# A fused attention stage: v as the stationary operand, pairs of query tiles, and probabilities scaled before they are turned

## The reference, cut to what matters

```python
s = einsum('bqhd,bkhd->bhqk', q, k) * ATT_SCALE
s = where(mask, s + cq - ck, -inf)            # causal; c: running sums of log forget values
o = einsum('bhqk,bkhd->bqhd', softmax(s), v)
...
merged = sigmoid(g_att) * (att @ w_pa) + sigmoid(g_ssm) * (y_ssm @ w_pb)
x = x + merged @ w_out                        # then an MLP
```

## Time and profile before

| what | value |
|---|---|
| median of 3 executions | 2892.29 us (2890.13 to 2892.56) |
| the profiled execution, its own time | 2892.2 us |
| its span, first to last instruction | 2890.4 us |
| mean granted TensorE clock | 0.982 of full |
| PE busy | 2782.0 us (96%) |
| DVE, ACT, POOL busy | 1653.6, 902.5, 251.4 us |
| attention stage | from about 400 to 1314 us of the span |
| branches stage | from about 1696 to 1930 us |

### The profile page before, as it was taken

The page is one execution under the profiler, slowest core; times in us unless marked ns, Lnnn a source line. Parts: engine busy times, 40 slices in busy tenths (PEclk is TensorE's granted clock), DMA queues, the critical chain, the costliest instruction groups (busy, mean ns, idle before and its releaser), DMA issues. The chain is left out here.

```text
span 2890.4 us, 48919 instructions
## 1 busy us (share of the span) xinstructions
PE 2782.0 (96%) x19338; PEld 2711.1 (94%) x19338; DVE 1653.6 (57%) x3203; ACT 902.5 (31%) x2161; POOL 251.4 (9%) x379
## 2 busy tenths in 40 slices
PE   6998979999999999997999989998989999999999
PEld 5997979999999999997999989998989999999999
DVE  4336337667667676676898854464373444344434
ACT  4223325444444444442434331121231111111110
POOL 0000000000000000003555520000000000000000
PEclk8999989999999999998999999999989999999999
DMA  3222232132222231325888863343121111111112
GB/s 115 90 90 56 76 90 91 44 100 78 72 86 82 74 93 52 91 73 135 208 198 207 204 188 116 111 138 123 63 104 55 48 45 44 44 45 44 47 67 95
DMA packets 339091, 273.38 MB, mean 95 GB/s; under 512 B 111824, under 2 KB 315216, under 8 KB 338736
## 3 DMA queue, kind: packets, MB, share of 16 engines
q1 hardware_dynamic: 338864, 270.26, 32.5%
HBM read 197.90 MB, written 72.28 MB: 93 GB/s over the span
## 5 line engine op out<-in xcount | busy, mean ns | idle before, releaser
L401 PE MATMUL banks<-w_hi,xn_hi 128*128 128x256 f32 x1440 | 405.0, 286 | 8.4 <-DVEq L357 5.0
L401 PE MATMUL banks<-w_lo,xn_hi 128*128 128x256 f32 x1440 | 402.0, 284 | 0.0
L404 PE MATMUL banks<-xn_hi,w_hi 128*128 128x352 f32 x1152 | 380.0, 330 | 0.0
L404 PE MATMUL banks<-xn_hi,w_lo 128*128 128x352 f32 x1152 | 377.4, 328 | 0.0
L404 PE MATMUL banks<-xn_lo,w_hi 128*128 128x352 f32 x1152 | 376.8, 327 | 0.0
L401 PE MATMUL banks<-w_hi,xn_lo 128*128 128x256 f32 x1280 | 363.1, 284 | 0.0
L401 PEld LDWEIGHTS banks<-w_hi,xn_hi 128*128 128x128 f32 x1440 | 274.3, 191 | 10.0 <-DVEq L357 5.1
L401 PEld LDWEIGHTS banks<-w_lo,xn_hi 128*128 128x128 f32 x1440 | 273.9, 190 | 0.6
L1683 PE MATMUL banks<-h_hi,w_hi 128*128 128x352 f32 x768 | 248.9, 324 | 1.9 <-DVEq L1604 1.9
L1683 PE MATMUL banks<-h_hi,w_lo 128*128 128x352 f32 x768 | 248.7, 324 | 0.0
L1683 PE MATMUL banks<-h_lo,w_hi 128*128 128x352 f32 x768 | 248.7, 324 | 0.0
(11 more groups left out here) (281 smaller groups left out, 6219.8 us busy)
## 6 DMA issues: line engine op xcount, KB each, us to landing
w_raw<-in_w_in SPq DMA_DIRECT2D x44, 1024.0 KB, 5.5
scratch_xbc<-att_co SPq DMA_DIRECT2D x32, 512.0 KB, 2.6
ssd_ab<-scratch_acum SPq DMA_DIRECT2D x64, 256.0 KB, 6.0
br_g<-scratch_gates SPq DMA_DIRECT2D x72, 176.0 KB, 2.5
scratch_gates<-hand_tanh SPq DMA_DIRECT2D x48, 176.0 KB, 5.1
scratch_z<-att_z_stage SPq DMA_DIRECT2D x64, 128.0 KB, 1.9
ssd_xbc<-scratch_xbc SPq DMA_DIRECT2D x64, 128.0 KB, 3.3
ssd_xbc<-scratch_xbc SPq DMA_DIRECT2D x128, 64.0 KB, 3.7
```

The lines of the kernel that those rows point to most:

```text
L401: ins = self.nc.tensor.matmul(self.bank(n, P, PW), x[:, k, t * P:(t + 1) * P], w[:, k, :], start=first, stop=end)
L404: ins = self.nc.tensor.matmul(self.bank(n, P, TT), w[:, k, m * P:(m + 1) * P], x[:, k, r * TT:(r + 1) * TT], start=first, stop=end)
```

## The change

The turned probabilities become the moving operand, and v_hl the stationary one, so that one load of v serves two query tiles. The unit of work is now a pair of query tiles (u = 0 to 3: tiles 2u and 2u + 1; u = 4, LASTU, is tile 8 alone). For a pair the blocks of both tiles are turned into one bank: four transposes to a full group (2 key blocks by 2 tiles), three to the diagonal one. The product comes out turned, [128, 256] for a pair: rows 0 to 63 are the high part of v, rows 64 to 127 the low one; ACT copies one half and DVE adds the other (64 partitions). As the row sum now lies along the free dimension of the output, it can't be applied there: POOL multiplies `pr` by it in place before the turning, after DVE has inverted it. A projection tile is cut in three parts (8 matmuls each), and a unit has three slots with the numbers of parts in `share`. att_d becomes [D, T], and branches reads its blocks without transposes.

```diff
-        size = len(passes) // parts
-        for c in range(part * size, (part + 1) * size):
+        for c in range(part * len(passes) // parts, (part + 1) * len(passes) // parts):
...
+        if s == 0:
+            sp.dma_start(self.blocks(u), self.att_d[:, tokens].rearrange("(k p) t -> p k t", p=P)).then_inc(self.rows_loaded[j], 16)
...
-                sp.wait_ge(turned, 2 * (u - 2))
+                if u - handed.ROWS < ST:
+                    sp.wait_ge(t_lo, 2 * (u - 2))
+                else:
+                    sp.wait_ge(turned, 2 * (u - 2 - ST))
...
-            for u in range(HEAD):
-                turn(u)
...
+                    if u < ST:
+                        bank = handed.blocks(u)[:, blocks, :]
...
+    prep_slot = {(1, 1): K0, (1, 2): QA, (3, 1): K1, (3, 2): QB, (LASTU, 1): KS}
...
+        share = {0: (3, 2, 1), 1: (3, 2, 1), 2: (2, 3, 3), 3: (2, 3, 1), 4: (2, 2, 1)}
...
+        def early(u):
+
+            return u != 2
...
+                elif g < u:
+                    for j in range(2):
+                        cols = slice(j * 2 * P, (j + 1) * 2 * P)
+                        mm(out, vt(2 * g + j), p_hi[:, cols], start=g + j == 0, stop=False)
+                        ins = mm(out, vt(2 * g + j), p_lo[:, cols], start=False, stop=False)
+                else:
+                    both, second = slice(0, 2 * P), slice(2 * P, 3 * P)
+                    mm(out, vt(2 * u), p_hi[:, both], start=u == 0, stop=False)
+                    mm(out[:, P:2 * P], vt(2 * u + 1), p_hi[:, second], start=False, stop=False)
+                    mm(out[:, P:2 * P], vt(2 * u + 1), p_lo[:, second], start=False, stop=False)
+                    ins = mm(out, vt(2 * u), p_lo[:, both], start=False, stop=True)
...
+            for x, (h, u) in enumerate(units):
+                hn, nxt = following(h, u)
+                for g in range(min(2, ngroups[u])):
+                    turn(h, u, g)
+                if nxt:
+                    scores(hn, nxt[0])
+                stream_parts(h, u, 0)
+                if early(u) and len(nxt) == 2:
+                    scores(hn, nxt[1])
+                for g in range(min(2, ngroups[u])):
+                    product(x, h, u, g)
+                for g in range(2, ngroups[u]):
+                    turn(h, u, g)
+                for g in prepared(h, u, 1):
+                    prep(h + 1, g)
+                stream_parts(h, u, 1)
+                if not early(u) and len(nxt) == 2:
+                    scores(hn, nxt[1])
+                for g in range(2, ngroups[u]):
+                    product(x, h, u, g)
+                for g in prepared(h, u, 2):
+                    prep(h + 1, g)
+                stream_parts(h, u, 2)
...
+                act.wait_ge(pv, x + 1)
...
+                nc.scalar.activation(o[x % OR][:, 0:w], out_bank[halves[(x + 1) % 2], 0:w], ACT.Copy).then_inc(o_low_made, 1)
...
+                pool.wait_ge(inverted, e + 1)
+                nc.gpsimd.tensor_scalar(y, y, rinv[e % 2][0:m, :], None, ALU.mult).then_inc(p_scaled, 1)
...
+            def invert(h, s):
+                e, m = h * ST + s, rows_of(s)
+                dve.wait_ge(s_exp, e + 1)
+                if e >= 2:
+                    dve.wait_ge(p_scaled, e - 1)
+                nc.vector.reciprocal(rinv[e % 2][0:m, :], rsum[e % 2][0:m, :]).then_inc(inverted, 1)
...
+            for x, (h, u) in enumerate(units):
+                hn, nxt = following(h, u)
+                probs_lo(h, u, 0)
+                if nxt:
+                    top_score(hn, nxt[0])
+                if ngroups[u] > 1:
+                    probs_lo(h, u, 1)
+                tile_ends(h, u, 0)
+                if ngroups[u] <= 2 and nxt:
+                    invert(hn, nxt[0])
+                if early(u) and len(nxt) == 2:
+                    top_score(hn, nxt[1])
+                for g in range(2, ngroups[u]):
+                    probs_lo(h, u, g)
+                if ngroups[u] > 2:
+                    invert(hn, nxt[0])
+                for g in prepared(h, u, 1):
+                    make_lo(h + 1, g)
+                if early(u) and len(nxt) == 2:
+                    invert(hn, nxt[1])
+                tile_ends(h, u, 1)
+                if not early(u) and len(nxt) == 2:
+                    top_score(hn, nxt[1])
+                    invert(hn, nxt[1])
+                for g in prepared(h, u, 2):
+                    make_lo(h + 1, g)
+                add_out(x)
+                tile_ends(h, u, 2)
...
-    q_d, att_d = scratch("q", [T, D]), scratch("att", [T, D])
+    q_d, att_d = scratch("q", [T, D]), scratch("att", [D, T])
```

More of the change, by code:

```diff
@@ L1708, in attention_z_xbc @@
     nkeys = [P * (s + 1) for s in range(NT)] + [SAMPLE]
[L1709 to L1712, removed]
+    ngroups = [u + 1 for u in range(LASTU)] + [1]
+    first_group = [sum(ngroups[:u]) for u in range(UN + 1)]
+    NG = first_group[UN]
     K0, QA, K1, QB, KS = range(5)
     PREP = 5
-    prep_step = {3: K0, 4: QA, 7: K1, 8: QB, 0: KS}
+    SEQ = [K0, QA, K1, QB, KS]
+    prep_slot = {(1, 1): K0, (1, 2): QA, (3, 1): K1, (3, 2): QB, (LASTU, 1): KS}
     B_SCORES, B_TURNED, B_PREP, B_OUT, B_TILES = 0, 2, 4, 5, (6, 7)
@@ L1754, in attention_z_xbc @@
+        tile = lambda n: (n // stream.slots, n % stream.slots, n // stream.slots == ROUNDS - 1)
+        PARTS = 3
+        FIRST = 3
         total = ROUNDS * stream.slots
[L1755 to L1762, removed]
@@ L1764, in after, with ends @@
-        def after(h, s):
-            return (h, s + 1) if s + 1 < ST else (h + 1, 0)
+        share = {0: (3, 2, 1), 1: (3, 2, 1), 2: (2, 3, 3), 3: (2, 3, 1), 4: (2, 2, 1)}
+        parts, at = {}, FIRST * PARTS
+        for h, u in units:
+            for slot in range(3):
+                end = min(at + share[u][slot], total * PARTS)
+                parts[h, u, slot] = range(at, end)
+                at = end
+        assert at == total * PARTS
+        def ends(h, u, slot):
+            return [tile(p // PARTS) for p in parts[h, u, slot] if p % PARTS == PARTS - 1]
@@ L1767, in q_tile, with turned_width, group_no @@
+        def turned_width(u, g):
+            return 3 * TS if u == LASTU else 3 * P if g == u else 4 * P
+        def group_no(h, u, g):
+            return h * NG + first_group[u] + g
         def q_tile(s):
@@ L1850, in _ @@
                 load_bias(0, g)
[L1851 to L1866, removed]
+            for n in range(FIRST):
+                stream.sp(sp, *tile(n))
+            for x, (h, u) in enumerate(units):
+                if u == 0 and h + 1 < H:
+                    load(h + 1)
+                for slot in range(3):
+                    for i, j, last in ends(h, u, slot):
+                        stream.sp(sp, i, j, last)
+                    if slot == 1 and x:
+                        store(x - 1)
+                if h + 1 < H:
+                    if u == 0:
+                        load_bias(h + 1, K0)
+                    elif u == 1:
+                        load_bias(h + 1, QA)
+                    elif u == 3:
+                        for g in (K1, QB, KS):
+                            load_bias(h + 1, g)
+            store(U - 1)
             for j in range(OR):
-                sp.wait_ge(o_stored[j], 16 * (E // OR))
+                sp.wait_ge(o_stored[j], 16 * (U // OR))
             z.finish(sp)
@@ L1943, in product, with stream_parts @@
+                if g == ngroups[u] - 1:
                     ins.then_inc(pv, 1)
+            def stream_parts(h, u, slot):
+                for p in parts[h, u, slot]:
+                    i, j, _ = tile(p // PARTS)
+                    stream.pe_part(pe, i, j, p % PARTS, PARTS)
             xbc.start_pe(pe, out_bank)
@@ L2116, in _ @@
[L2116 to L2130 removed]
+            make_lo(0, KS)
```

329 lines of the change are left out of this document (180 added, 149 removed).

## The result

The changed kernel takes 2952.43 us in the median of four runs (2949.76 to 2957.62), the kernel before 2891.73 (2890.13 to 2892.56): a ratio of 1.0212, 95% interval 1.0200 to 1.0224. The forecast was 2866 with a range of 2840 to 2904, so it is wrong in sign and the time lies outside the range. The profiled execution took 2957.62 us (span 2955.8, against 2890.4 before).

The account below looks back on a forecast made before the run. PE's issue was taken to bound the attention stage. 2892.2 - 49 (products) + 5 (cutting of tiles) - 6 (branches) + 24 (PE's waits for scaled probabilities) = 2866 us; range 2840 to 2904.

Parts of the forecast that it names:

- the price of two inputs: Far end for POOL's scaling in attention, from a two-input POOL operation: 2.28 us for 1024 columns.
- The chains and covers: In attention, steps from scores to scaled probabilities against PE's work meanwhile; the excess is waiting, 24 us in all.
- the lateness d: What DVE's lateness and its port sharing with POOL add to a chain: taken as 1.0 us, between 0 and 2.6.
- the chain ahead of unit 3: Scores to scaling of tile 7 (1024 keys): 3.97 us, against 4.30 of PE work in x panels, 3.34 in z.
- unit 1's tile: Tile 5, 768 keys: scores to scaling takes 4.54 us, against PE work of 5.6 or 4.6.
- Rival 3: POOL's scaling, at two inputs' price, makes PE wait before turn in units 2 and 3: 2903 us, chance 0.21.
- keep their place: Stores of z and of the convolution stay behind DVE's epilogues, so DMAs don't bound the kernel; no size given.
- the products: Attention's probability-times-v matmuls on PE: 8.42 us a head removed, 5.35 added, 49 us less over 16 heads.
- the branches: Start of the branches stage: the first matmul needs three loaded tiles and no transposes; 6 us less.
- The cutting of tiles: More returns from attention matmuls to the projection, 240 slots for 144 steps: 5 us more, bounds 0 and 10.
- the forecast's own interval: Whole kernel at 2852 to 2882 us, for DVE lateness and sharing of 0.4 to 1.6 us; chance 0.42.
- Rival 4: In attention's products the moving columns set the price: 14 us added instead of 49 saved, 2929 us; chance 0.03.

Follow-up runs that it names:

- run 1: Changed kernel, but POOL copies the probabilities in place instead of multiplying them (division left out of the result): 2885.97 us, 0.9983 of the kernel before.
- run 8: Changed kernel, but POOL multiplies by the constant 1.0 instead of each row's inverse (division left out of the result): 2948.80 us, a single run.
- run 4: Changed kernel plus twelve useless 256-column matmuls on PE ahead of the first turn of units 2 and 3: 2936.83 us, 1.0162 of the kernel before.
- run 5: Changed kernel with tiles 5 and 7 of each head scaled on DVE, the rest on POOL: 2894.15 us, 1.0007 of the kernel before.
- run 6: Changed kernel, tiles 5 and 7 scaled on DVE, next head's eight loads behind the first two slots' weight loads in SP's order: 2885.50 us, 0.9978.
- run 10: Changed kernel without any scaling (division left out of the result), SP's order as in run 6: 2869.16 us, 0.9917 of the kernel before.
- run 9: Changed kernel, SP's order as in run 6, every pair's second tile and the running tile scaled on DVE, the rest on POOL: 2882.51 us, 0.9961.

## Why the prediction was wrong

1. **What failed is one step: "The scaling has one tensor input and a scalar per row, so I take the copy's price".** That gave 1.03 us for 1024 columns; 2.84 was measured, and even the end that I kept, the price of two inputs (2.28), was too low. Like was put to like by counting inputs, while what tells the operations apart here is whether POOL computes or only copies: runs 1 and 8 show 1.04 and 2.77 us for the same shape with the same one tensor input. The Trainium skill, GPSIMD Engine Reference, section Engine selection, says that elementwise work on GpSimd is about twice as slow for two inputs and that "1-input is roughly line-rate". Here the copy is near that (1.04 us, against 0.75 for DVE's scaling of the same shape; no run copies on DVE); the multiplication isn't: 2.84 against 0.75 on DVE is 3.8 times, and the measurement decides. The nearest row in kind, a multiplication on POOL, was the one of two inputs, and it stood in the trace.
2. **The chains and covers themselves were right, and the lateness d was put too high.** With 2.84 in place of 1.03 the chain ahead of unit 3 is 3.97 + 1.81 = 5.78 us, against covers of 4.30 and 3.34: waits of 1.48 and 2.44 with d = 0. The timeline has 1.53 to 2.03 in the eight heads with x panels there, and 2.43 to 3.20 in the eight with z panels. So d was 0.25 on average for that tile, at most 0.8, and not 1.0. For unit 1's tile the same gives 4.54 - 0.82 + 2.20 = 5.92, and with POOL's measured mean of 2.91 6.63, against 5.6 and 4.6; over the stage that would be 13 and 24 us of waits, and 18.4 were measured. Part of what I had put into d sits there in POOL's own duration (2.20 to 2.91 us), and it depends on what DVE runs at the moment when POOL begins. DVE's instructions got longer too: the taps 1390 ns on average, 1316 before.
3. **Rival 3 is what happened**, by its mechanism and at its place: the largest waits are PE's for `p_scaled` ahead of `turn` in units 2 and 3. It was to decide from 3.1 us a head; POOL's waits are 68.7 / 16 = 4.3. Its time of 2903 was 50 too low because of the price, and because of the next point.
4. **The clock was left out of the waits' price.** It is some 37 us, by the windows; run 4 gives 26 to 30 back by filling part of the gaps. I had read the half clock in the trace of before, at one gap at the start of the branches, and priced it there only. It belonged to the waits of the stage as well, the 1.63 us and 2.33 us that I had in the sum and in rival 3.
5. **Had POOL cost what I took, the time would be 2886, not 2866** (run 1). About half of the missing 20 are waits: PE's come to 41 us there, 34 more than before, where the forecast had 24. The rest, some 8 us, is clock again (22 us at the low level in which PE works, against 6). A part of it is the late weights: I wrote that the stores "keep their place", and didn't follow SP's order past the eight loads of a head. Moving these was worth 8.6 us between runs 5 and 6; beside run 1 it wasn't tried. The small waits that run 10 shows are the other part.
6. **Right:** the products (-49, measured -53), the branches (-6, measured -6.2), and that neither ACT's own load nor the stores bound the changed kernel. The cutting of tiles (+5) wasn't measured by itself; the stage's sum, 41 less where the products give 53, leaves 12 to it and to all else. Rival 4 is refuted by the stage's sum for the products; the starts 0.12 apart for 256 columns are its own price and don't speak against it. One sum was off: d = 1.6 gives 2885 as the end of the forecast's own interval, not 2882; nothing hangs on it.

What stays open: how the 19 us of the floor divide between the cutting into slots and the lag of maximum and exp in z panels, and whether another sharing of the projection's parts would win them back; that wasn't tried.

## What to carry to other kernels

Price a moved operation by a row of the same engine doing the same kind of arithmetic, and where there is none, by the dearest row of that engine, not by the row with the same number of inputs; here even that was too low (2.28 for 2.84). Where an engine that was off the path is put into a chain, write out the chain against its cover at that price, and then add to each wait what a row of the trace shows PE's clock to lose behind one of that length. Follow each in-order queue past the work that was moved around it: loads of weights behind eight others cost 8.6 us here, while the two ways of sharing tiles between DVE and POOL (runs 6 and 9) differ by 3.0, which the intervals don't separate.

## What was not expected of the hardware

- POOL multiplies 1024 columns of 128 rows in 2.84 us by a scalar per row and in 2.77 by a constant, and copies them in 1.04; DVE multiplies them in 0.75, ACT in 1.15.
- A kernel with 46 us more work for PE was 15.6 us faster, because the work lay in waits behind which the granted clock had fallen to 0.50, once for 6.4 us. After the four waits of 1.53 us ahead of unit 3 the windows show no fall; after the sixteen of 1.9 us and more for POOL they show one, but for a single wait of 2.01 us.
- Two runs with the same sum of PE's waits (46.6 and 46.7 us) differed by 8.6 us, about what their mean granted clocks differ by (0.9788 and 0.9815).
- The same POOL scaling of 768 columns took 2.20 us when no tap or split ran on DVE at its start, and 2.50 to 3.92 when one did. The copy got longer by the same 0.71 us on average. Where POOL began first it kept its time (2.84 for 1024 columns in all 16 heads), and DVE's split took 1.24 us beside it instead of 0.68.
